# The meta tokens' rows of the token-major projections in plain fp32, four partial sums in the quarters of the array

## What is computed

```
first block, two layers:
  xn = rms_norm(h, attn_norm)
  gq, gk, gv, gr, glr, fq, fk, fv, ff = split(xn @ w_in)     # 1024 x 3096
  gated linear attention over chunks: the 16 meta tokens are chunk 0,
     u = sum_s diag(b_end / b_s) k_s v_s^T,  S_c = diag(decay_c) S_{c-1} + u_c,  o_t = q_t S_c
  forgetting softmax attention over all keys up to t, meta tokens included
  h = h + [o_gla, o_fox] @ w_out;  h = h + conv_ffn(rms_norm(h))
second block, one layer:
  sparse attention over the best-scored keys with v = (rmsnorm(h) @ w)[v part],
  a short convolution, gates, and a gated MLP
```

## Time and profile before

| | us |
|---|---|
| median of 3 runs | 2383.76 (2382.78 to 2384.36) |
| the profiled execution, its time | 2382.39 |
| its span, first to last instruction | 2381.2 |
| TensorE busy | 2330.6 |
| VectorE busy | 1294.2 |
| ScalarE busy | 901.7 |

### The profile page before, as it was taken

The page is one execution under the profiler, slowest core; times in us unless marked ns, Lnnn a source line. Parts: engine busy times, 40 slices in busy tenths (PEclk is TensorE's granted clock), DMA queues, the critical chain, the costliest instruction groups (busy, mean ns, idle before and its releaser), DMA issues.

```text
span 2381.2 us, 36337 instructions
## 1 busy us (share of the span) xinstructions
PE 2330.6 (98%) x15276; PEld 2082.9 (87%) x15276; DVE 1294.2 (54%) x2259; ACT 901.7 (38%) x1534; POOL 33.2 (1%) x62
## 2 busy tenths in 40 slices
PE   8999999999999999899999999999999999999998
PEld 7798889999998798899899878988899877888886
DVE  4355476536643455566456556777654455443443
ACT  5245454324433255544234443322244444321222
POOL 0000010000000000100000000000000000000000
PEclk9999999999999999999999999999999999999999
DMA  3121132322322221233223222222212122232231
GB/s 133 54 90 52 32 105 91 105 80 90 101 68 67 81 68 43 62 98 101 88 87 102 89 80 72 84 86 88 98 66 68 62 90 96 95 106 82 95 115 48
DMA packets 57189, 197.58 MB, mean 83 GB/s; under 512 B 8337, under 2 KB 10803, under 8 KB 57027
## 3 DMA queue, kind: packets, MB, share of 16 engines
q1 hardware_dynamic: 55107, 189.86, 24.3%
q0 software_dynamic: 1344, 4.36, 0.6%
q10 hardware_dynamic: 576, 1.05, 0.1%
HBM read 193.11 MB, written 2.13 MB: 82 GB/s over the span
## 4 chain that ended last, share of the span: by engine, by line
PE 93%; DVE 4%; ACT 2%; issue 1%; DMA 0%; SPq 0%; DVEq 0%; ACTq 0%
PE G L916 76%; PE G L951 7%; PE X L951 2%; PE X L1082 1%; PE X L1126 1%; PE X L1207 1%; PE X L1105 1%; DVE wL L1624 1%; PE X L1025 1%; PE X L1192 1%; DVE aL L1631 1%; PE X L1177 1%; DVE hT L1737 0%; PE X L1164 0%; ACT wH L1241 0%
## 5 line engine op out<-in xcount | busy, mean ns | idle before, releaser
L916 PE MATMUL G<-aH,wH 128*128 128x264 f32 (+3 forms) x3248 | 822.5, 317 | 30.9 <-DVE wL L1624 16.8
L916 PE MATMUL G<-aL,wH 128*128 128x264 f32 (+3 forms) x3248 | 795.4, 309 | 0.0
L916 PE MATMUL G<-aH,wL 128*128 128x264 f32 (+3 forms) x3248 | 794.3, 308 | 0.0
L1241 ACT ACTIVATE wH<-raw 128x512 fp32r<-128x512 f32 (+4 forms) x495 | 393.0, 812 | 697.0 <-PE G L916 638.3
L916 PEld LDWEIGHTS G<-aH,wH 128*128 128x128 f32 (+1 forms) x3248 | 529.1, 189 | 76.4 <-issue 29.7
L1624 DVE TENSOR_TENSOR wL<-raw,wH 128x512 fp32r<-128x512 f32 (+4 forms) x495 | 455.0, 931 | 252.4 <-ACT wH L1241 251.2
L916 PEld LDWEIGHTS G<-aH,wL 128*128 128x128 f32 (+1 forms) x3248 | 526.2, 188 | 30.5
L916 PEld LDWEIGHTS G<-aL,wH 128*128 128x128 f32 (+1 forms) x3248 | 527.2, 188 | 27.6 <-issue 0.2
L1737 DVE TENSOR_TENSOR hT<-G,hT 128x528 f32<-128x528 f32 (+1 forms) x88 | 61.5, 699 | 232.9 <-PE G L916 232.9
L916 PE MATMUL G<-hidH,wH 128*128 128x264 f32 (+1 forms) x528 | 140.8, 321 | 1.4 <-DVE hidL L1821 1.4
L916 PE MATMUL G<-hidL,wH 128*128 128x264 f32 (+1 forms) x528 | 141.2, 322 | 0.0
(11 more groups left out here) (279 smaller groups left out, 2478.4 us busy)
## 6 DMA issues: line engine op xcount, KB each, us to landing
raw<-weights SPq DMA_DIRECT2D x272, 512.0 KB, 3.3
raw<-weights SPq DMA_DIRECT2D x48, 704.0 KB, 4.0
raw<-weights SPq DMA_DIRECT2D x16, 384.0 KB, 3.0
negc<-sums POOLq DMA_DIRECT2D x16, 264.0 KB, 4.6
raw<-weights SPq DMA_DIRECT2D x16, 128.0 KB, 2.0
out_t<-hT SPq DMA_DIRECT2D x8, 256.0 KB, 2.1
hT<-x_t ACTq DMA_DIRECT2D x4, 256.0 KB, 4.8
hT<-x_t SPq DMA_DIRECT2D x4, 256.0 KB, 6.4
```

What stands on the lines that cost most here:

```text
L916: done = e.matmul(m.G[g][0:M, bank, 0:n], a[:, k, 0:M], b[:, k0 + k, lo - t0:lo - t0 + n], start=(k == 0 and c == 0), stop=(k == nk - 1 an ...
L1241: e.activation(m.wH[:, i % NW, c], m.raw[:, r, c], ACT.Copy).then_inc(s.w_hi, 1)
```

## The change

The j = 0 step of a token-major chunk no longer takes the split operands. A new small tensor `xm` holds the first 32 token columns of the normalised-gain activations unsplit; ScalarE writes it, eight activations of 128 x 32 (128 x 16 for vv) per norm, in `sq` of the attention norms and in `prepmid`. The stationary operand of j = 0 is `xm` (128 x 32), the moving one is `raw`, the unsplit weights, 256 columns at a time. The four products of a chunk (k blocks times halves of 256 columns) go into four different quarters of 32 PSUM partitions of bank 3, which are four 32-column quarters of the array, and each quarter accumulates over the chunks of the group on its own. In the last chunk ScalarE copies quarters 1 to 3, scaled, to partitions 0 to 15 of `tmpn`, and VectorE adds quarter 0 and the three copies into the output (two operations for 512 columns, where two quarters belong to each half; three for gk). `rtok` is copied three more times so that it lies beside each quarter. SP's load into a `raw` buffer also waits until the j = 0 products of the chunk in it are done. New semaphores: tm_raw, tm_shift, tm_meta, meta_in.

```diff
         if c == 0:
             if j == 0:
                 if n > 1:
-                    e.wait_ge(s.tm_act, 3 * (n - 1) - 2)
+                    e.wait_ge(s.tm_meta, n - 1)
...
+        wr = m.raw[:, i % NR, 0:1024].rearrange("p (k n) -> p k n", n=cols)
         t0 = TOK[j][0]
         for kk in range(nk):
             k = c * nk + kk
             if j == 0:
                 wait_weights(i, kk)
+                if c == kk == 0:
+                    e.wait_ge(s.meta_in, 8 * RTOK["mid",] if name == "vv" else 8 * RTOK["attn", role[1]])
+                for half in range(cols // 256):
+                    t = kk * cols // 256 + half
+                    done = e.matmul(out[32 * t:32 * t + 32, 0:256], m.xm[:, k, :], wr[:, kk, 256 * half:256 * half + 256],
+                                    start=(c == 0), stop=(c == 8 // nk - 1))
+                    done.then_inc(s.tm_raw, 1)
+                continue
             for q, (a, b) in enumerate(((m.aH, wh), (m.aL, wh), (m.aH, wl))):
                 done = e.matmul(out[:, 0:cols], a[:, k, t0:t0 + 128], b[:, kk, :], start=(k == 0 and q == 0),
                                 stop=(k == 7 and q == 2))
...
@@ act_program, sq
+        if key[0] == "attn":
+            e.activation(m.xm[:, j, :], m.hT[:, j, 0:32], ACT.Copy, scale=m.vc(key, j)).then_inc(s.meta_in, 1)
...
@@ act_program, tmout
+        if j == 0:
+            e.wait_ge(s.rtok, RTOK["mid",] if role[0] == "vv" else RTOK["attn", role[1]])
+            e.wait_ge(s.tm_raw, 4 * TM_CHUNK[i])
+            if n > 1:
+                e.wait_ge(s.tm_meta, n - 1)
+            if role[0] == "vv":
+                e.wait_ge(s.z_in, 8)
+            for t in range(1, 4):
+                r = slice(32 * t, 32 * t + 16)
+                e.activation(meta_part(m, t), X[r, 3, 0:256], ACT.Copy, scale=m.rtok[r, 0:1]).then_inc(s.tm_shift, 1)
+            return
...
+def meta_part(m, t):
+    return m.tmpn[0:16, 1 + (t == 3), 256 * (t == 2):256 * (t == 2) + 256]
...
@@ dve_program, rtok
+        e.tensor_copy(m.rtok[32:48, 0:1], X[0:16, 2, 0:1]).then_inc(*own.one())
+        e.tensor_copy(m.rtok[64:80, 0:1], X[0:16, 2, 0:1]).then_inc(*own.one())
+        e.tensor_copy(m.rtok[96:112, 0:1], X[0:16, 2, 0:1]).then_inc(s.rtok, 1)
...
@@ dve_program, tmout
+        if j == 0:
+            out, r = token_major_out(m, role, 0)[0:16], m.rtok[0:16, 0:1]
+            if role[0] in ("fv", "vv"):
+                e.wait_ge(s.vzero if role[0] == "vv" else s.kzero, 1 if role[0] == "vv" else role[1] + 1)
+            e.wait_ge(s.tm_raw, 4 * TM_CHUNK[i])
+            e.wait_ge(s.tm_shift, 3 * n)
+            first = 2 if w == 512 else 1
+            e.scalar_tensor_tensor(out=out[:, 0:256], in0=X[0:16, 3, 0:256], scalar=r, in1=meta_part(m, first), op0=ALU.mult,
+                                   op1=ALU.add).then_inc(*own.one())
+            if w == 512:
+                e.tensor_tensor(out[:, 256:512], meta_part(m, 1), meta_part(m, 3), ALU.add).then_inc(s.tm_meta, 1)
+            else:
+                e.wait_ge(own.sem, own.n)
+                e.tensor_tensor(out, out, meta_part(m, 2), ALU.add).then_inc(*own.one())
+                e.wait_ge(own.sem, own.n)
+                e.tensor_tensor(out, out, meta_part(m, 3), ALU.add).then_inc(s.tm_meta, 1)
...
@@ sp_program, load
         if i >= NR:
             e.wait_ge(s.w_lo, SPLIT_DONE[i - NR][-1])
+            if i - NR in TM_CHUNK:
+                e.wait_ge(s.tm_raw, 4 * TM_CHUNK[i - NR])
```

More of the change, by code:

```diff
@@ L686, in __init__ @@
         self.go, self.gn, self.tm_mm = new("go"), new("gn"), new("tm_mm")
+        self.tm_raw = new("tm_raw")
         self.ft, self.fs = new("ft"), new("fs")
@@ L693, in __init__ @@
         self.rms_ln, self.act = new("rms_ln"), new("act")
-        self.tm_act = new("tm_act")
+        self.tm_act, self.tm_shift, self.meta_in = new("tm_act"), new("tm_shift"), new("meta_in")
         self.k_hi, self.q_hi = new("k_hi"), new("q_hi")
@@ L707, in __init__ @@
         self.psum, self.tm_dve, self.rtok, self.mid = new("psum"), new("tm_dve"), new("rtok"), new("mid")
+        self.tm_meta = new("tm_meta")
         self.mid_sum = new("mid_sum")
@@ L842 @@
 TM_LAST = [i for i, role in enumerate(ROLE) if role[0] in TOKEN_MAJOR and (i + 1 == len(PLAN) or ROLE[i + 1][:-1] != role[:-1])]
+TM_CHUNK = {i: n + 1 for n, i in enumerate(i for i, role in enumerate(ROLE) if role[0] in TOKEN_MAJOR)}
 TM_NTH = {ROLE[i][:-1]: n + 1 for n, i in enumerate(TM_LAST)}
@@ L905, in mm @@
                 n, first = token_major[g]
-                e.wait_ge(s.tm_act, 3 * n - (1 if first else 0))
+                e.wait_ge(s.tm_act, 2 * n - (1 if first else 0))
                 e.wait_ge(s.tm_dve, 2 * n - (1 if first else 0))
@@ L954, in tm @@
             done.then_inc(s.chunk, 1)
-        elif k == 7:
+        elif k == 7 and j:
             done.then_inc(s.tm_mm, 1)
@@ L1198, in do @@
         if n == 0:
-            e.wait_ge(s.tm_act, 3 * TM_NTH["vv", 1])
+            e.wait_ge(s.tm_act, 2 * TM_NTH["vv", 1])
             e.wait_ge(s.tm_dve, 2 * TM_NTH["vv", 1])
+            e.wait_ge(s.tm_meta, TM_NTH["vv", 1])
         else:
@@ L1290, in prepmid @@
         operand_high(m.aH[:, j, 0:NM], meta, m.vc("mix2", j))
+        e.activation(m.xm[:, j, 0:NM], meta, ACT.Copy, scale=m.vc("mix2", j)).then_inc(s.meta_in, 1)
         one, both = (m.tmpn[:, 0, NM:L], m.rbc) if j == 0 else (m.tmpn[:, 1, NM:L], m.tmpn[:, 2, :])
@@ L1320, in tmout @@
         else:
[L1321 to L1332, removed]
+            e.wait_ge(s.tm_mm, 3 * (n - 1) + j)
+        e.activation(token_major_out(m, role, j), token_major_bank(m, i, j)[:, 0:w], ACT.Copy,
+                     scale=m.rtok[:, j:j + 1]).then_inc(s.tm_act, 1)
     def rest(i, q):
@@ L1690, in rtok @@
         e.wait_ge(s.rtok_mm, RTOK[key])
-        e.tensor_copy(m.rtok[:, 0:5], X[:, 2, 0:10].rearrange("p (j c) -> p j c", c=2)[:, :, 0]).then_inc(s.rtok, 1)
-    def tmout(i, j):
[L1694 to L1701, removed]
+        e.tensor_copy(m.rtok[:, 0:5], X[:, 2, 0:10].rearrange("p (j c) -> p j c", c=2)[:, :, 0]).then_inc(*own.one())
@@ new lines, in rtok @@
+        e.wait_ge(own.sem, own.n)
+        e.tensor_copy(m.rtok[32:48, 0:1], X[0:16, 2, 0:1]).then_inc(*own.one())
+        e.tensor_copy(m.rtok[64:80, 0:1], X[0:16, 2, 0:1]).then_inc(*own.one())
+        e.tensor_copy(m.rtok[96:112, 0:1], X[0:16, 2, 0:1]).then_inc(s.rtok, 1)
+    def tmout(i, j):
+        role, n, w = ROLE[i], TM_NTH[ROLE[i][:-1]], WIDE[i]
+        if j == 0:
[12 more added lines that the diff above has]
+                e.tensor_tensor(out, out, meta_part(m, 2), ALU.add).then_inc(*own.one())
+                e.wait_ge(own.sem, own.n)
+                e.tensor_tensor(out, out, meta_part(m, 3), ALU.add).then_inc(s.tm_meta, 1)
+        elif j % 2:
+            e.wait_ge(s.tm_mm, 3 * (n - 1) + j)
+            if j == 1:
+                e.wait_ge(s.rtok, RTOK["mid",] if role[0] == "vv" else RTOK["attn", role[1]])
+            e.tensor_scalar(token_major_out(m, role, j), token_major_bank(m, i, j)[:, 0:w], m.rtok[:, j:j + 1], None,
+                            ALU.mult).then_inc(s.tm_dve, 1)
```

16 lines of the change are left out of this document (10 added, 6 removed).

## The result

The changed kernel takes 2365.62 us in the median of 4 runs (2364.56 to 2367.04), the kernel before 2383.27 on the same chip (2381.74 to 2384.36, 4 runs). The ratio is 0.9927, with a 95% interval of 0.9910 to 0.9944: 17.65 us less, where 18.0 were forecast. The profiled execution has a time of 2364.56 and a span of 2363.3; before it was 2382.39 and 2381.2, so the traces differ by 17.9 us. The forecast of the total was right. Its parts were not all right: a loss that nobody had priced and a gain that is in no part of the sum nearly cancelled, and that the total is hit so closely is luck. What the parts measured is what the rest of this text is about.

What follows compares the result with a forecast made beforehand. TensorE was taken to bound the kernel, busy 98% of the span. Terms -18.8 + 0.4 + 0.4 = -18.0 us took 2382.39 to 2364.4, plus 1.37 for the median: 2365.8, range 2362.5 to 2379.5.

Steps and rivals of the forecast that it cites:

- The burst: A chunk's j = 0 products on TensorE: two rounds of simultaneous instructions, 0.72 us instead of 1.39; 28 save 18.8 us.
- The wait for the low half: TensorE's wait for VectorE's split weights at j = 0: given no price; no new wait over 0.5 us expected.
- xm at the start of layer 0: Eight small ScalarE activations between the squares of layer 0's first norm: 0.05 us exposed a turn, +0.4 us in all.
- The state product in fv: TensorE's state product at fv's last chunk waits for VectorE's later update: about 0.2 us a layer, +0.4 us.
- The sums' room: Adding the quarters at a group's end takes 2.5 us; the next group needs bank 3 after 5.6, leaving 2.6 us spare.
- Rival (d): Products overlap but the quarters' sums come late, so TensorE waits for bank 3 or a state: 2369 us, chance 0.06.
- the two costs that did not appear: The +0.4 us for xm in layer 0 and the +0.4 us for the state product in fv.
- (a): Two tiles at a time, or one quarter out of step: four rounds, 1.14 us per j = 0 step, 2377.6 us; chance 0.12.
- (b): Only one product's low half overlaps the next one's high half: five rounds, 1.35 us, 2383.5 us, no change; chance 0.08.
- (c): No overlap among the four quarters' products, because of a shared read path: eight rounds, 2401.1 us, slower; chance 0.10.

Runs made afterwards that it cites:

- the repetition: The changed kernel run once more with no edit, beside other follow-up kernels on one chip: 2365.78 us, ratio to the kernel before 0.9927.

## Why the prediction was right, and where it was not

**The burst, forecast at 0.72 us.** Right, and close. Two rounds, as forecast; four quarters do what L1126's two halves do. What it was made of differed a little: 0.24 for the first round and 0.33 for the second with the way out, together 0.57, where 2 x 0.21 + 0.2 = 0.62 stood; entry 0.10 as forecast; and 0.12 on the first product behind the burst, which was not foreseen. In the ledger a regular burst saves 0.62 in vv, and in the layers, where the next instruction is often plain fp32 already, 0.70 in the mean. With what the irregular ones lost put back (1.55 and 0.21 in vv, 0.17 in gk in each layer), it is 6.95 + 6.94 + 4.97 = 18.9 us, where 18.8 were forecast.

**The wait for the low half, forecast at nothing.** This is the step that failed. The prediction priced the burst by its length and kept the old step's waits as they were, but a step that is half as long asks for its second operand earlier, and three small copies ahead of it on VectorE deliver it later. 2.1 us of the 18.9 were lost there, 1.55 of them in one burst, and 16.8 remain. The version without that wait shows it by removing it. The prediction expected no new wait of over 0.5 us of TensorE in the token-major stretches; there is one, of 0.93.

**xm at the start of layer 0, forecast at +0.4.** It costs 0.12 once, and nothing in each turn. VectorE's sums of squares, before and after:

```profile
16.21 5.58 DVE L1678 TENSOR_TENSOR tmpn<-tmpn 128x528 f32<-128x528 f32 x7
```

```profile
16.32 5.58 DVE L1707 TENSOR_TENSOR tmpn<-tmpn 128x528 f32<-128x528 f32 x7
```

They run back to back for the same 5.58 us, since VectorE sets this pace. I had added a recorded duration (0.65 for a square) to a distance between starts (0.22 for xm). A square with another instruction close behind holds ScalarE for only 0.54:

```profile
16.41 0.63 ACT L1291 ACTIVATE tmpn<-hT 128x528 f32<-128x528 f32 x1
16.94 0.31 ACT L1285 ACTIVATE xm<-hT,vec 128x32 f32<-128x32 f32 x1
17.15 0.63 ACT L1291 ACTIVATE tmpn<-hT 128x528 f32<-128x528 f32 x1
```

0.54 and 0.21 make 0.75, under VectorE's 0.81. Only the first turn starts 0.11 later, which is the +0.12 of the ledger.

**The state product in fv, forecast at +0.4.** No stall. The state products write alternating banks, and each waits for the update before the last (`if c >= 2`, a count of c - 1), not for the last, as the description of `gst` above has it. In the changed kernel it starts 0.61 us before VectorE's update ends (timeline of all engines):

```profile
110.28 1.47 DVE L1987 SCALAR_TENSOR_TENSOR S<-S,dec,X 64x128 f32<-64x128 f32 x4
...
111.14 1.13 PE L1041 MATMUL X<-gv,gk 64*128 64x256 f32 x4
```

The same could have been read from the code of the kernel before. Its update ran 115.82 to 117.30 with the product at 117.80, and TensorE was busy without a gap up to that product: what set its time was TensorE's order of steps, not a wait.

**The sums' room, forecast at 2.6 us.** Right in effect (the sums stall nothing in the changed kernel), wrong in size and in place. Behind gv it is 1.3 us, set by the next chunk's second low half and not by bank 3, and behind vv 0.3. The sums also end later than forecast: 3.2 us after the burst's start (73.82 to 77.02) where 0.26 + 2.5 stood. Rival (d) was nearer than its text said.

**The clock.** 1.3 us of the 17.9 are from no part of the sum. Both kernels have a wait of 2.6 us for activations in layer 0, near which the granted clock falls to 0.50 (1.2 GHz): from 237.4 to 244.2 us before, and from 233.0 to 236.4 after, half as long. Before and after (columns as in the earlier trace rows; the clock is the third number from the right):

```profile
236.00:244.00 8.00, 6.04 (x26) 5.09 (x27) 5.06 (x15) 3.78 (x9) 0.00 (x0) 0.59 0.01 2
```

```profile
228.00:236.00 8.00, 5.42 (x33) 4.63 (x32) 5.98 (x16) 4.37 (x10) 0.00 (x0) 0.81 0.01 2
```

Whether the change does this to every execution is open. Stretches of this kind moved by about a microsecond between kernels whose work there is the same, and the repetition's profiled span is 2364.9 against 2363.3. So the two costs that did not appear (0.8, less the 0.12) and the clock (1.34) paid for the lost 2.10: 18.86 - 2.10 - 0.12 - 0.11 + 1.34 = 17.87, the 0.11 being the small shifts of the table. A slip in the prediction's own range is without effect: with 0.77 saved in each burst and no costs beside it, its lower end is 2383.76 - 21.6 = 2362.2, not 2362.5.

**The rivals.** (a), (b) and (c) fall with the four simultaneous starts, and the runs with one and two quarters show that the prices of (a) and (c) were right for a chip that worked so. By the Trainium skill's picture of the buses ("TensorE: Matmul & The Clock Gate", part 2) the last quarter's bus is faulty and unsupported; all four quarters run in step here, in 24 of 28 bursts and in all of them once the wait is gone. By part 3 of the same page, completions of concurrent tiles that each increment a semaphore are serialised at some 26 ns each and one increment would save three of them a burst, an estimate of 2.2 us over 28 bursts by the page's figure. The run with one increment shows no difference (2365.67 against 2365.62). The measurement decides for this use, in which the next products don't wait for those increments.

## What to carry to other kernels

A product with few stationary columns can run four at a time in quarters of the array, in plain fp32 too; price it as a fixed part plus rounds (0.57 + 0.21 x (rounds - 2) us for 256 columns here, and 0.2 around it), and gather several into one visit, because the fixed part is paid for each. When a step is made shorter, go through its waits again: its later operands are now wanted earlier, small additions on the engine that makes them count, and a wait that belonged to the old operands may not be needed for the new ones. For ScalarE and VectorE in a row, add distances between starts, never recorded durations, and look for the room of a delayed engine in everything queued behind it, not only in the one that waits by name.

## What the hardware did that was not expected

- Four plain fp32 products in four quarters start within 0.02 us of each other and cost exactly the rounds: 0.57, 0.98 and 1.84 us for the same eight instructions in four, two and one quarters.
- The first 512-column product behind such a burst is followed after 0.33 to 0.35 us instead of 0.23, each time.
- Sixteen instructions in one burst keep their pace: sets at 0.24, 0.22 and 0.22 us, with no limit seen in how many are under way.
